# Router products inside the mixer's output projection, the root mean square applied per token afterwards, and token rows by identity products, in a two-layer diffusion backbone

## The reference, cut to what matters

```python
x = x + g1 * mix                                  # mix = attn_out(...) or z @ w_out + b_out
h = modulate(rmsnorm(x, norm_ffn), sh2, sc2)      # x * rsqrt(mean(x*x) + EPS) * gain * (1 + sc2) + sh2
g_logits = t @ wg + bg                            # t = h as 384 rows; 4 groups
e_logits = einsum('nd,dge->nge', t, we) + be      # 32 experts
# top group, then the two best experts in it; softmax weights; 32 expert networks of 1024 -> 256 -> 1024
x = x + g2 * hierarchical_moe(h, ...)
```

## Time and profile before

| what | value |
|---|---|
| median of 3 runs | 1300.36 us (1297.46 to 1305.96) |
| profiled execution, its own time | 1303.83 us |
| its span, first to last instruction | 1302.0 us |
| around the span | 1.8 us |
| mean granted TensorE clock | 0.921 of full speed |
| TensorE busy with matmuls | 1107.0 us, 85% of the span |
| VectorE, ScalarE, GpSimd busy | 473.2, 257.0 and 132.7 us |
| weights and data moved | 324.37 MB |

### The profile page before, as it was taken

One profiled execution on the slowest core, in us unless ns is written; L12 is line 12 of the kernel. 1 busy time (PEld: TensorE's weight loads), 2 busy tenths in 40 slices (PEclk: granted clock), 3 DMA queues, 4 the chain that ended last, 5 costly groups with the idle time before them and its releaser, 6 DMA issues.

```text
span 1302.0 us, 14521 instructions
## 1 busy us (share of the span) xinstructions
PE 1107.0 (85%) x5453; PEld 583.0 (45%) x5453; DVE 473.2 (36%) x1001; ACT 257.0 (20%) x498; POOL 132.7 (10%) x127
## 2 busy tenths in 40 slices
PE   5789888997899789999969999989974988877864
PEld 3334555557444233443435565748862422222223
DVE  2336457316033212333163336775260111111116
ACT  2211145213233121333222111000131100000001
POOL 0000000000222022221010001230002011111000
PEclk8889889996899889999989999999967999999987
DMA  8986886604599864999981020404050699999933
GB/s 331 384 312 231 259 259 259 259 24 166 193 383 404 334 237 176 398 402 402 389 318 39 1 97 1 189 38 194 27 216 18 255 416 414 414 416 410 406 158 138
DMA packets 95681, 324.37 MB, mean 249 GB/s; under 512 B 19337, under 2 KB 35137, under 8 KB 78822
## 3 DMA queue, kind: packets, MB, share of 16 engines
q1 hardware_dynamic: 78384, 304.22, 60.5%
q0 software_dynamic: 10016, 12.26, 2.7%
q10 hardware_dynamic: 7190, 6.66, 1.5%
HBM read 315.85 MB, written 30.04 MB: 266 GB/s over the span
## 4 chain that ended last, share of the span: by engine, by line
PE 64%; DMA 16%; DVE 7%; SPq 4%; issue 4%; ACT 3%; ACTq 1%; POOL 1%; POOLq 0%; DVEq 0%
PE bank L848 16%; DMA ring<-in_moe_w_up 12%; PE bank L995 10%; PE bank L862 5%; PE bank L1034 3%; PE bank L780 3%; PE bank L574 3%; PE bank L609 3%; PE bank L668 2%; PE bank L1023 2%; PE bank L981 2%; PE bank L795 2%; DMA work<-token_vectors,curx 2%; PE bank L631 1%; PE bank L592 1%
## 5 line engine op out<-in xcount | busy, mean ns | idle before, releaser
L848 PE MATMUL bank<-ring,work 128*64 128x512 f32 x1120 | 271.9, 642 | 44.4 <-issue 39.0
L848 PEld LDWEIGHTS bank<-ring,work 128*64 128x64 f32 x1120 | 83.4, 147 | 224.4 <-issue 220.7
L995 PE MATMUL bank<-hT,ring 128*128 128x384 f32 x384 | 128.0, 494 | 5.3 <-ACT hT L1135 5.3
L862 PE MATMUL bank<-ring,work 128*64 128x512 f32 x560 | 127.9, 598 | 4.2 <-DVE work L1627 1.5
L1639 DVE SCALAR_TENSOR_TENSOR work<-bank,work 128x256 f32<-128x256 f32 x32 | 15.5, 483 | 259.6 <-ACT work L1229 259.6
L995 PEld LDWEIGHTS bank<-hT,ring 128*128 128x128 f32 x384 | 74.0, 194 | 58.0 <-issue 9.7
L862 PEld LDWEIGHTS bank<-ring,work 128*64 128x64 f32 x560 | 37.1, 136 | 72.9 <-issue 62.3
L1229 ACT ACTIVATE work<-bank 128x256 f32<-128x256 f32 x32 | 12.2, 383 | 254.3 <-PE bank L848 254.3
L1651 DVE COPY work<-bank 128x512 f32<-128x512 f32 x32 | 22.1, 690 | 105.3 <-PE bank L862 105.3
L574 PE MATMUL bank<-ring,condS 128*32 128x256 f32 x768 | 50.3, 418 | 10.5 <-DMA ring<-in_w_ada 6.5
L1126 ACT ACTIVATE sq<-xT 128x384 f32<-128x384 f32 x40 | 20.8, 522 | 170.1 <-DVE xT L1752 85.2
(11 more groups left out here) (246 smaller groups left out, 1452.3 us busy)
## 6 DMA issues: line engine op xcount, KB each, us to landing
ring<-in_moe_w_gate SPq DMA_DIRECT2D x32, 2048.0 KB, 16.3
ring<-in_moe_w_up SPq DMA_DIRECT2D x32, 2048.0 KB, 21.9
ring<-in_moe_w_down SPq DMA_DIRECT2D x32, 2048.0 KB
ring<-in_w_ada SPq DMA_DIRECT2D x24, 2048.0 KB, 11.7
ring<-in_hy_w_in SPq DMA_DIRECT2D x6, 2048.0 KB, 20.5
filter_spectra<-work ACTq DMA_DIRECT2D x8, 768.0 KB
work<-expert_rows SPq DMA_DIRECT2D x16, 384.0 KB, 6.3
ring<-filter_spectra SPq DMA_DIRECT2D x2, 3072.0 KB, 12.3
```

The lines of the kernel that those rows point to most:

```text
L848: last = mm(bank[2][WIN * j:WIN * (j + 1), :], gt[:, k, WIN * j:WIN * (j + 1)], gu[:, :, j, k, :], start=(k == 0), stop=(k == KD - 1))
L862: last = mm(bank[b + hf][WIN * j:WIN * (j + 1), :], AT[:, k, WIN * j:WIN * (j + 1)], dn[:, j, k, hf * HALF:(hf + 1) * HALF], start=(k == 0 ...
L995: last = mm(bank[n % 2][:, 0:T], w[:, k, (n % 4) * P:(n % 4 + 1) * P], hT[:, k, :], start=(k == 0), stop=(k == KD - 1))
```

## The change

1. **Router products per block.** Right after the addition of block k, VectorE writes `hT[k] = xT[k] * amul` (`router_x`, two operations). TensorE makes that block's share of the logits (`logit_mm`, 3 products, 6 records) two rounds behind, right after `norm_sum`, into banks 4 to 6. Layer 1's output projection uses banks 0 and 1 in place of 4 and 5. The full-width reciprocal, the multiplications of lines 1387 and 1395 and ScalarE's modulation of line 1135 are gone for the two router norms (n = 1 and 3); they stay for the mixers' norms.
2. **The shift apart.** What the shift adds to the logits does not depend on the token: VectorE adds it up over the blocks (`shift_sums`, 16 linked operations of 128 x 36 or so many), TensorE sums over the partitions (`shift_mm`, after round 1), and `shift_bias` adds the router's bias. `shift_mm` also turns the shifts into rows, which go through DRAM to one partition (`shrow`; `shift_row` on SP, three small DMAs in its queue between the early loads and the wait for the projection's last round).
3. **Root mean square per token.** ScalarE's root stays (a dummy Sqrt is put ahead of the squares). Three products of one partition x 128 tokens with one element turn it into a column per token (bank 3), VectorE takes the reciprocal of 128 x 3 (`rstdc`), and the logits come from one operation for each group of tokens: raw logits times `rstdc` plus bias.
4. **Token rows by products.** Each of the six groups is now a product of one partition (root of the token's mean square) with the 512 shifts of `shrow`, and four products of `hT` with the identity added to it in the same bank; ScalarE's copy multiplies by `rstdc`. Three banks are used in turn. Groups 0 to 2 stand ahead of the placement products, groups 3 to 5 behind them.
5. **Order in the router.** After the one-hot matrix of pair 0 come the running numbers (`cum_set`), then the one-hot matrix of pair 1, then the combine weights and `slots_set`. Before, `slots_set` stood ahead of the running numbers.

Renamed semaphores and buffers moved within the work area are left out of the diff.

```diff
+        shD = [nc.dram_tensor(f"shift_rows{l}", [2 * KD, P], F32, kind="Internal").ap() for l in range(DEPTH)]
...
+        def shift_row(sp, l):
+            sp.wait_ge(sem("shift_set"), 2 * l + 2)
+            sp.dma_start(shD[l], strow).then_inc(sem("shrow_in"), 16)
+            sp.wait_ge(sem("shrow_in"), 48 * l + 16)
+            for c in range(2):
+                sp.dma_start(shrow[:, c * D:(c + 1) * D].rearrange("p (k i) -> p k i", k=KD),
+                             shD[l].rearrange("(a k c) i -> c a k i", a=1, k=KD)[c]).then_inc(sem("shrow_in"), 16)
...
             load_gu(sp, 0, 0, (0,))
+            shift_row(sp, 0)
             sp.wait_ge(sem("mix0_mm"), KD)
...
             load_dn(sp, 1, 0)
+            shift_row(sp, 1)
             sp.wait_ge(sem("mix1_mm"), KD)
...
+            def logit_mm(l, k):
+                if k == 0:
+                    pe.wait_ge(sem("rout_in"), 16 * 9)
+                pe.wait_ge(sem("xa_set"), 2 * (KD * l + k + 1))
+                for c in range(TC):
+                    last = mm(bank[4 + c][:, 0:NG + NE], hT[:, k, c * P:(c + 1) * P], rout[:, l, k, :],
+                              start=(k == 0), stop=(k == KD - 1))
+                if k == KD - 1:
+                    last.then_inc(sem("logit_mm"), 1)
+
+            def shift_mm(l):
+                pe.wait_ge(sem("shift_set"), 2 * l + 1)
+                for c in range(2):
+                    last = mm(bank[7][:, 64 * c:64 * c + NG + NE], ones, shacc[:, c, :], start=True, stop=True)
+                tr(bank[7][0:2 * KD, 256:256 + P], ada[:, l, 3].rearrange("p k c -> p (k c)"), ident).then_inc(sem("row_mm"), 1)
...
                 last.then_inc(sem("mix0_mm"), 1)
+                if m == 1:
+                    shift_mm(0)
                 if m >= 2:
                     norm_sum(1, m - 2)
+                    logit_mm(0, m - 2)
             for k in (KD - 2, KD - 1):
                 norm_sum(1, k)
+                logit_mm(0, k)
 
 
-                pe.wait_ge(sem("rout_in"), 16 * 9)
-                for k in range(KD):
-                    wait_h(n_norm, k)
-                    for c in range(TC):
-                        last = mm(bank[c][:, 0:NG + NE], hT[:, k, c * P:(c + 1) * P], rout[:, l, k, :],
-                                  start=(k == 0), stop=(k == KD - 1))
-                last.then_inc(S_("logit_mm"), 1)
-
-                for g in range(2 * TC):
+                pe.wait_ge(sem("rt_done"), n_norm + 1)
+                for c in range(TC):
+                    last = mm(bank[3][:, c:c + 1], rstd[0:1, c * P:(c + 1) * P], ones[0:1, 0:1], start=True, stop=True)
+                last.then_inc(sem("row_mm"), 1)
+
+                def token_rows(g):
                     c, hf = divmod(g, 2)
-                    if g >= 2:
-                        pe.wait_ge(S_("htok_set"), B_("htok_set") + g - 1)
+                    if g == 0:
+                        pe.wait_ge(sem("shrow_in"), 48 * (l + 1))
+                        pe.wait_ge(sem(f"mix{l}_done"), 2 * KD)
+                    if g >= 3:
+                        pe.wait_ge(S_("htok_set"), B_("htok_set") + g - 2)
+                    b = bank[(2, 0, 1)[g % 3]]
+                    at = (1 if c else 0) * D + hf * HALF
+                    mm(b[:, :], rstd[0:1, c * P:(c + 1) * P], shrow[:, at:at + HALF], start=True, stop=False,
+                       skip_group_check=True)
                     for k in range(4):
-                        last = tr(bank[4 + g % 2][:, k * P:(k + 1) * P], hT[:, 4 * hf + k, c * P:(c + 1) * P], ident)
+                        last = mm(b[:, k * P:(k + 1) * P], hT[:, 4 * hf + k, c * P:(c + 1) * P], ident,
+                                  start=False, stop=(k == 3), skip_group_check=True)
                     last.then_inc(S_("htok_mm"), 1)
 
+                for g in range(3):
+                    token_rows(g)
                 pe.wait_ge(S_("mask_set"), B_("mask_set") + 1)
                 for c in range(TC):
                     mm(bank[7][:, 256:256 + NE], ones, m_all[:, c], start=(c == 0), stop=(c == TC - 1))
@@ -812,6 +854,8 @@
                         last = mm(bank[7][:, c * 64:c * 64 + NE], C["before"] if c2 == c else ones,
                                   m_all[:, c2], start=(c2 == 0), stop=(c2 == c))
                 last.then_inc(S_("place_mm"), 1)
+                for g in range(3, 6):
+                    token_rows(g)
...
-                        last = mm(bank[4 + m % 2][:, lo:hi], wout[:, k, m * P:(m + 1) * P], st[:, 2, k, a0:a1],
+                        last = mm(bank[m % 2][:, lo:hi], wout[:, k, m * P:(m + 1) * P], st[:, 2, k, a0:a1],
                                   start=(k == 0), stop=(k == KD - 1))
                 last.then_inc(sem("mix1_mm"), 1)
+                if m == 1:
+                    shift_mm(1)
                 if m >= 2:
                     norm_sum(3, m - 2)
+                    logit_mm(1, m - 2)
             for k in (KD - 2, KD - 1):
                 norm_sum(3, k)
-            pe.wait_ge(sem("mix1_done"), 2 * KD)
+                logit_mm(1, k)
             moe(1, 3)
 
...
+                fn(idle[:, :], eps_col[:, :], ACT.Sqrt)
                 squares(n_norm, f"mix{l}_done")
-                modulate(n_norm, l, 1)
+                act.wait_ge(S_("lg_set"), B_("lg_set") + 1)
 
                 for g in range(2 * TC):
                     c, hf = divmod(g, 2)
                     act.wait_ge(S_("htok_mm"), B_("htok_mm") + g + 1)
                     dst = hTok[:, c, :].rearrange("p (k a) -> p a k", k=8)[:, 64 * hf:64 * (hf + 1), :]
-                    fn(dst, bank[4 + g % 2].rearrange("p (a k) -> p a k", k=8), ACT.Copy).then_inc(S_("htok_set"), 1)
-
-                act.wait_ge(S_("gsub_set"), B_("gsub_set") + 1)
+                    fn(dst, bank[(2, 0, 1)[g % 3]].rearrange("p (a k) -> p a k", k=8), ACT.Identity, scale=rstdc[:, c:c + 1])\
+                        .then_inc(S_("htok_set"), 1)
+
+                act.wait_ge(S_("soft_in"), B_("soft_in") + 1)
                 fn(gx.rearrange("p a b -> p (a b)"), gx.rearrange("p a b -> p (a b)"), ACT.Exp).then_inc(S_("gexp"), 1)
-                act.wait_ge(S_("dv_set"), B_("dv_set") + 1)
+                act.wait_ge(S_("soft_in"), B_("soft_in") + 2)
...
+            def shift_sums(l):
+                for c in range(2):
+                    for k in range(KD):
+                        s = ada[:, l, 3, k, c:c + 1]
+                        if k == 0:
+                            link(v.tensor_scalar(shacc[:, c, :], rout[:, l, k, :], s, None, ALU.mult))
+                        elif k < KD - 1:
+                            link(v.scalar_tensor_tensor(shacc[:, c, :], rout[:, l, k, :], s, shacc[:, c, :], ALU.mult, ALU.add))
+                        else:
+                            last = v.scalar_tensor_tensor(shacc[:, c, :], rout[:, l, k, :], s, shacc[:, c, :], ALU.mult, ALU.add)
+                last.then_inc(sem("shift_set"), 1)
+
+            def shift_bias(l):
+                dve.wait_ge(sem("row_mm"), 2 * l + 1)
+                v.tensor_copy(strow, bank[7][0:2 * KD, 256:256 + P]).then_inc(sem("shift_set"), 1)
+                for c in range(2):
+                    last = v.tensor_tensor(cbias[:, c, :], bank[7][:, 64 * c:64 * c + NG + NE], rbias[:, l, :], ALU.add)
+                link(last)
+
+            def router_x(l, k):
+                dve.wait_ge(sem(f"mix{l}_done"), 2 * (k + 1))
+                for c, (lo, hi) in enumerate(SPANS):
+                    v.tensor_scalar(hT[:, k, lo:hi], xT[:, k, lo:hi], amul[:, l, 1, k, c:c + 1], None, ALU.mult)\
+                        .then_inc(sem("xa_set"), 1)
+
+            dve.wait_ge(sem("rout_in"), 16 * 9)
+            dve.wait_ge(sem("oT_set"), KD)
+            shift_sums(0)
             for k in range(KD):
                 add_mix(k, bank[k % 2], sem("mix0_done"), ada[:, 0, 2], sem("mix0_mm"))
+                router_x(0, k)
+                if k == 1:
+                    shift_bias(0)
...
-                dve.wait_ge(S_("logit_mm"), B_("logit_mm") + 1)
+                dve.wait_ge(sem("row_mm"), 2 * l + 2)
+                link(v.reciprocal(rstdc, bank[3][:, 0:TC]))
+                dve.wait_ge(sem("logit_mm"), l + 1)
                 for c in range(TC):
-                    v.tensor_tensor(lg[:, c], bank[c][:, 0:NG + NE], rbias[:, l, :], ALU.add).then_inc(S_("lg_set"), 1)
+                    v.scalar_tensor_tensor(lg[:, c], bank[4 + c][:, 0:NG + NE], rstdc[:, c:c + 1], cbias[:, 1 if c else 0, :],
+                                           ALU.mult, ALU.add).then_inc(S_("lg_set"), 1)
                 dve.wait_ge(S_("lg_set"), B_("lg_set") + TC)
...
-                for q in range(2):
+                def pair_rows(q):
...
-                dve.wait_ge(S_("gexp"), B_("gexp") + 2)
...
-                v.tensor_copy(pay[:, :, :, 2].bitcast(F32), wck).then_inc(S_("slots_set"), 1)
-
+                pair_rows(0)
                 c1, c2 = cnt[:, 0:PAIRS + 1], cnt[:, 32:32 + PAIRS + 1]
...
```

(31 more changed lines are left out.)

36 lines of the change are left out of this document (18 added, 18 removed).

## The result

| | before | after |
|---|---|---|
| median | 1302.48 us (4 runs, 1297.46 to 1305.96) | 1316.31 us (4 runs, 1313.75 to 1317.85) |
| profiled execution, its span | 1303.83, 1302.0 us | 1313.75, 1311.9 us |
| mean granted clock | 0.921 | 0.916 |

The ratio is 1.0107, 95% interval 1.0067 to 1.0148. 1286 was forecast.

What follows compares the result with a forecast made beforehand. Each layer's stretch from projection to the start of its experts was taken to count in full. Gains of 8.5 us (layer 0) and 6.0 (layer 1) take the profiled 1303.83 to 1289.3, the median to 1286; 8 in 10 range 1277 to 1296.

Steps and rivals of the forecast that it cites:

- What bounds the kernel: Projection's end to experts' start counts in full: 41.88 us to layer 0's gate and up, 33.41 to layer 1's slots_set.
- Projection: Added narrow products lengthen each layer's output projection by 4.9 us: six blocks at 0.675, shift_mm 0.56, switching back 0.3.
- Rival D: Narrow products between the projection's wide ones cost 0.217 us each; gain only 3.9 us, 1296.5 us; chance 0.10.
- Tail: After the projection's end, last logits, root and column products let the logit sums start at 4.9 us instead of 18.70.
- Token groups: On TensorE around placement, each group takes 1.82 us, 0.43 per record of the one-partition product; three take 5.46.
- Rival B: TensorE's clock is down from the tail on, through groups and gather; 2.5 us slower, 1302.9 us; chance 0.05.
- The exponentials, "just hidden": ScalarE's exponentials, behind the last token copy, are ready near 20.8 us against a need near 21, before slots_set.
- Gather and its start: After token groups 3 to 5, the gather starts at 19.1 us and takes 5.76 at full clock instead of 8.01.
- rival A: Clock falls in the placement stage, groups 3 to 5 take 3.06 us each; gain 10.8 us, 1289.6 us; chance 0.12.
- Rival C: Clock survives the pause before layer 0's pair 0; first product 6.9 us instead of 10.10; -17.4, 1283.0 us; chance 0.18.
- The sum: Layer 0 gains 8.5 us and layer 1 gains 6.0, together -14.5 us over the whole kernel.

Runs made afterwards that it cites:

- E1: Changed kernel with the one-partition product of each token group spread over all 128 partitions, shifts divided by 128; 1287.12 us, ratio 0.9883.
- E8: E7's kernel with GpSimd's fill of the gather buffers moved behind the last router_x; 1283.74 us, ratio 0.9873.
- E4: E1's kernel with the product over 32 partitions in place of 128; 1313.76 us, ratio 1.0093.
- E5: E1's kernel with the product over 64 partitions in place of 128; 1315.0 us in a single run.
- E6: E1's kernel with the undivided shift row on partition 0 and zeros on the other 127; 1290.21 us, ratio 0.9917.
- E11: Changed kernel, product still over one partition, with only the two exponentials moved ahead of the copy of group 3; 1305.8 us, ratio 1.0038.
- E7: E1's kernel with the exponentials ahead of group 3's copy, and combine weights and slots_set back ahead of the running numbers; 1285.87 us, ratio 0.9886.
- E9: E1's kernel unchanged, timed again in more rounds; 1288.94 us, ratio 0.9909.
- E2: Changed kernel without the one-partition product of each token group, so token rows lack the shift; 1285.28 us, ratio 0.9874.

## Why the prediction was wrong, by its own steps

**What bounds the kernel: right.** Each layer's stretch counted in full. In the changed kernel layer 0's 6.4 us longer stretch, less 1.5 us that the first gate and up product got shorter, moved layer 1's projection by 4.3 (654.56 us from the one projection to the other instead of 650.23); the 0.6 us between 4.9 and 4.3 were not followed up. Layer 1's 6.6 came on top, and the rest of the span stayed the same (307.9 against 308.3). The sum is 10.4, as between the two profiled executions from the start of layer 0's projection to the end (1067.9 against 1057.5 us); the whole spans differ by 9.9, the medians by 13.8. E1 gives the same bookkeeping with the other sign: -9.3, -4.4 and +1.4.

**Projection: the price nearly right, the count wrong.** 3.8 us instead of 4.9: an inner round grew from 5.81 to 6.48, and six logit records take 0.59 in it, not 0.675. But most of the difference is a slip of counting: the prediction put six blocks ahead of the projection's end and three behind it, nine of eight. With products two rounds behind, five stand ahead, and five times 0.675 is 0.7 us less. Rival D is refuted: narrow products between wide ones run at the full-clock price.

**Tail: right in layer 0.** 5.1 against 4.9. In layer 1 it was 5.7: VectorE's last `router_x` took 2.04 us beside GpSimd's fill, which the prediction did not have. With the fill later (E8) it is 5.1 there too (937.46 - 932.37).

**Token groups: the step that failed.** The prediction priced the product of one partition at 0.43 us a record "as time goes by columns in all rows", and took 1.82 for a group. At full clock that is near: E1 has 1.75 over 128 partitions, and the changed kernel's own first product of one partition, made before the clock fell, took 0.97 for its two records. In the half-clock groups the record takes 1.00, above the upper bound of 0.86. What was wrong is the clock itself. The prediction had half clock as its upper bound, took the full clock, and set the chance of a clock that stays down at 0.05, because in the old kernel it had risen during transposes with less to do. Those transposes use 128 partitions. E1, E4, E5 and E6 show that this is what counts here: groups at 1, 32 and 64 partitions hold TensorE busy and its clock at 0.50, at 128 they hold or lift it. All partitions alone are not enough either: the old logits ran over 128 of them, 36 columns wide, with TensorE busy throughout at 0.50.

**Rival B: the right mechanism, priced too low.** It began later than B had it, inside the first group and not in the tail. B forecast +2.5, measured is +10.4. It took half-clock records from a gather of 8.01 / 48 = 0.167, a mixture of both clocks; the identity record at half clock is 2.00 / 8 = 0.25 here, and the wide one 1.00 where B had 0.86. So a group cost 4.00 instead of 3.06. After the projection's end the groups of layer 0 were over at 30.6 instead of B's 27.6, and gate and up started at 44.4 instead of 39.8. In layer 1 B kept the path on VectorE and lost nothing to the exponentials; that was the second fault.

**The exponentials, "just hidden": the second step that failed.** They were to be ready near 20.8 against a need near 21, with the remark that each us lost in the groups would show here as well. It did: VectorE stood 6.63 us. The margin was wrong even at full clock: a copy takes 1.12 to 1.15 us, not the 0.97 of the old one, and E1 still has a wait of 1.47 us. E11 shows 6.4 us of layer 1's stretch to be this. E7 shortens that stretch by 4.4 us in E1's kernel, of which part is the order on VectorE; the two were not taken apart there.

**Gather and its start.** Its length is right at full clock: 5.60 against 5.76 in E1; 9.58 in the changed kernel. Its start is not: 21.7 us after the projection's end in E1, not 19.1. 1.5 us of that are rival A in a small form: the clock fell just behind the placement products, and group 3 took 3.26 us, where A had three groups at 3.06. Rival C came about in part: the clock was 1.00 at 330 to 335, and the gate and up product took 8.63 us instead of 10.10 (8.78 in E1), not C's 6.9.

**The sum.** The forecast was -14.5. With the clock kept up, E1 has -14.2 in the medians (1287.12 against 1301.27) and -12.4 in the profiled spans, counted from the start of layer 0's projection; repeated as E9 it is -11.4 in the medians. So most of the gain was there once the clock stayed up. That it comes so near the sum is in part luck: in E1 the projections are 1.1 us shorter than forecast in each layer, and the stretches behind them 1.7 us (30.19 against 28.5) and 2.8 us (25.3 against 22.5) longer.

## What to carry to other kernels

In this kernel a wide product over few partitions cost little by its own columns and much by what it did to the clock of all that followed. Give such a product all 128 partitions, with the operand spread over them or with zeros, where it stands in a stretch that must run at 2.4 GHz, and read the granted clock of the stretch afterwards. Price a stretch at each of the two clock levels with rows taken wholly at that level, and weigh the case that it comes out at the lower one by what the products are made of, not by how busy TensorE is. An operation said to be "just hidden" behind a queue wants its place in that queue looked at first: here two exponentials ahead of the last copies gave back 6.4 us of layer 1's stretch.

## What the runs showed of the hardware that had not been expected

- With TensorE busy all the time, groups whose wide product covers 1, 32 or 64 partitions ran at a granted clock of 0.50 (4.00 us a group), and with 128 partitions, also with 127 of them zeros, at 1.00 outside the dip behind the placement products (1.75 us). The clock had been 1.00 before, and fell within the first group. The Trainium skill ("TensorE: Matmul & The Clock Gate", Part 1) ties the clock to how busy TensorE has been, by which these groups should have run at 2.4 GHz; the measurement decides.
- Two VectorE operations of 128 x 128 and 128 x 256 elements took 2.04 us instead of 0.55 while GpSimd filled a tile (1.80 us), in both layers; with the fill moved behind them they took 0.55 (E8). The Trainium skill ("Advanced Engine Details and Errata", VectorE Performance Modes) says that GpSimd and VectorE's two-port modes block each other at the port that they share; this agrees, though no run shows in which mode the two operations ran.
- Identity products lifted the clock from 0.50 to 1.00 (E2), 24 records in 5.29 us. The old kernel's logits, 48 records of 36 columns over 128 partitions in 10.43 us without a gap, left it at 0.50.
